# Differential attention: the roots of the output norm reach all partitions through a row in DRAM instead of through TensorE, and the last two pairs of a head are normed in the next head

## What is computed

```
a = (p1 - lam * p2).astype(v.dtype)
o = jnp.einsum("bhqk,bhkd->bhqd", a, v)
...
y = xf * lax.rsqrt(jnp.mean(xf * xf, axis=-1, keepdims=True) + NORM_EPS)
o = rms_norm(o, subln_w) * (1.0 - lam_init)
```

## Time and profile before

| | |
|---|---|
| time, median of 3 runs | 3609.38 us (3599.21 to 3609.42) |
| the profiled execution, its own time | 3618.67 us |
| its span | 3616.9 us |
| mean granted TensorE clock | 0.964 of full speed |
| PE matmul busy | 3342.2 us (92%) |
| PE weight loads busy | 3084.3 us (85%) |
| DVE busy | 1868.7 us (52%) |
| ACT busy | 1185.8 us (33%) |
| POOL busy | 942.6 us (26%) |

### The profile page before, as it was taken

One profiled execution on the slowest core, in us unless ns is written; L12 is line 12 of the kernel. 1 busy time (PEld: TensorE's weight loads), 2 busy tenths in 40 slices (PEclk: granted clock), 3 DMA queues, 4 the chain that ended last, 5 costly groups with the idle time before them and its releaser, 6 DMA issues. The chain is left out here.

```text
span 3616.9 us, 51583 instructions
## 1 busy us (share of the span) xinstructions
PE 3342.2 (92%) x20797; PEld 3084.3 (85%) x20797; DVE 1868.7 (52%) x2655; ACT 1185.8 (33%) x2106; POOL 942.6 (26%) x726
## 2 busy tenths in 40 slices
PE   5898898998889999999988999999798999999997
PEld 4777777887789999999988777777598999999996
DVE  4555555555155554555545555565416545555454
ACT  3334344444232222122223555555413121222111
POOL 1122112222233322223233121221133322332221
PEclk8999999998899999999999999999899999999998
DMA  6333343113211111111112111101231111111101
GB/s 240 108 107 113 112 125 116 51 40 121 87 42 47 41 53 35 41 37 39 54 38 78 38 30 26 35 23 35 97 99 58 42 36 41 41 37 56 35 29 59
DMA packets 206659, 229.78 MB, mean 64 GB/s; under 512 B 30564, under 2 KB 173533, under 8 KB 205341
## 3 DMA queue, kind: packets, MB, share of 16 engines
q1 hardware_dynamic: 186973, 162.69, 14.8%
q10 hardware_dynamic: 11664, 42.47, 3.5%
q0 software_dynamic: 7856, 22.29, 1.7%
HBM read 181.79 MB, written 31.98 MB: 59 GB/s over the span
## 5 line engine op out<-in xcount | busy, mean ns | idle before, releaser
L205 PE MATMUL psum<-Hh,wh 128*128 128x384 f32 x3360 | 1142.2, 340 | 52.6 <-ACT Hh L377 14.7
L206 PE MATMUL psum<-Hh,wl 128*128 128x384 f32 x3360 | 1131.0, 337 | 0.0
L207 PE MATMUL psum<-Hl,wh 128*128 128x384 f32 x3360 | 1130.9, 337 | 0.0
L286 DVE SCALAR_TENSOR_TENSOR x<-psum,mod,x 128x384 f32<-128x384 f32 (+2 forms) x768 | 377.4, 514 | 684.6 <-PE psum L207 643.2
L205 PEld LDWEIGHTS psum<-Hh,wh 128*128 128x128 f32 x3360 | 636.6, 189 | 63.3 <-issue 35.5
L206 PEld LDWEIGHTS psum<-Hh,wl 128*128 128x128 f32 x3360 | 636.8, 190 | 0.0
L207 PEld LDWEIGHTS psum<-Hl,wh 128*128 128x128 f32 x3360 | 636.5, 189 | 0.0
L816 POOL TENSOR_TENSOR wl<-wr,wh 128x1024 fp32r<-128x1024 f32 x88 | 219.8, 2498 | 986.6 <-ACT wh L735 986.6
L766 ACT ACTIVATE ff_u<-psum 128x768 f32<-128x768 f32 x88 | 71.6, 814 | 1109.2 <-PE psum L207 1109.2
L205 PE MATMUL psum<-ff_ah,ff_dh 128*128 128x384 f32 x1056 | 365.1, 346 | 29.4 <-POOL ff_al L838 20.7
L964 DVE SCALAR_TENSOR_TENSOR ff_c<-ff_u,par,ff_c 128x1153 f32<-128x1153 f32 x176 | 377.4, 2144 | 15.8 <-DVE ff_c L961 5.2
(11 more groups left out here) (217 smaller groups left out, 4267.8 us busy)
## 6 DMA issues: line engine op xcount, KB each, us to landing
wr<-w_up SPq DMA_DIRECT2D x88, 512.0 KB, 3.9
ff_dr<-w_down SPq DMA_DIRECT2D x22, 1024.0 KB, 6.1
da_mw<-mod_w ACTq DMA_DIRECT2D x40, 512.0 KB, 3.9
wr<-mod_w ACTq DMA_DIRECT2D x40, 512.0 KB, 4.8
wr<-w_qkv_diff SPq DMA_DIRECT2D x24, 512.0 KB, 19.2
x<-x_save SPq DMA_DIRECT2D x16, 576.0 KB, 7.5
in_mw<-mod_w SPq DMA_DIRECT2D x8, 1024.0 KB, 12.2
Hh<-oh_save SPq DMA_DIRECT2D x14, 576.0 KB, 9.8
```

Source lines behind the costliest of these rows:

```text
L205: pe.matmul(out, w_hi, m_hi, start=start, stop=False)
L206: pe.matmul(out, w_lo, m_hi, start=False, stop=False)
L207: return pe.matmul(out, w_hi, m_lo, start=False, stop=stop)
L286: last = dve.scalar_tensor_tensor(g.x[:, m, lo:hi], g.PS[:, bank, lo - n * NB:hi - n * NB], g.mod[:, gate + m, cond:cond + 1], g.x[:, m, l ...
```

## The change

The "BC" products leave TensorE and the list of bank uses. In their place SP issues two transfers for each pair: `spread_out` writes the one or two columns of `r` from 128 partitions into a row of DRAM, token by token (`r_rows`, 4 bytes each), and `spread_in` reads that row of 1024 bytes back into the `y` buffer of every partition. `spread_in` waits until `spread_out` has landed, and SP, which issues in order, waits with it. `normalise` reads `o` and `y` in SBUF and writes `y` in place. The pairs 3 and 4 of a head are normed and stored in step 1 of the next head; those of the last head after its loop. `outputs` on ACT waits for the norm of two pairs before, or for the whole head before it in pairs 0 and 1.

```diff
+        g.r_rows = nc.dram_tensor("r_rows", [2, 2, P], F32, kind="Internal").ap()
...
-    PV_AT, ST_AT, BC_AT = {2: [0], 4: [1], 6: [2], 8: [3], 9: [4]}, {3: [0], 5: [1], 7: [2], 9: [3, 4]}, {4: [0], 6: [1], 8: [2], 9: [3, 4]}
+    PV_AT, ST_AT, Y_AT = {2: [0], 4: [1], 6: [2], 8: [3], 9: [4]}, {3: [0], 5: [1], 7: [2], 9: [3, 4]}, {5: [0], 7: [1], 9: [2]}
...
-            last = tiles + [("PV", 4), ("ST", 3), ("ST", 4)] + [("W+",)] * ahead2 + [("BC", 3), ("BC", 4)]
+            last = tiles + [("PV", 4), ("ST", 3), ("ST", 4)] + [("W+",)] * ahead2
...
-        u += [("BC", p) for p in BC_AT.get(s, [])]
...
+            def spread_out(h, p):
+                n, done = PAIRS[p][1], len(PAIRS) * h.index + p
+                sp.wait_ge(b.r_d, done + 1)
+                if done >= 2:
+                    sp.wait_ge(b.r_in, 16 * (done - 1))
+                sp.dma_start(g.r_rows[done % 2, 0:n].rearrange("i q -> q i"), b.r[:, p, 0:n],
+                             allow_slow_non_contiguous=True).then_inc(b.r_out, 16)
+
+            def spread_in(h, p):
+                n, done = PAIRS[p][1], len(PAIRS) * h.index + p
+                sp.wait_ge(b.r_out, 16 * done + 16)
+                sp.wait_ge(b.y_split, max(2 * (done - 1), 0) + Y0)
+                sp.dma_start(b.y[:, done % 2, 0:n * P],
+                             g.r_rows[done % 2, 0:n].rearrange("i q -> (i q)").partition_broadcast(P)).then_inc(b.r_in, 16)
...
                 if not ahead:
                     sp.wait_ge(b.y_out, 32 * len(PAIRS) * (HEADS - 1) + 16)
                     load_outputs(g, sp, b)
+                    for p in range(3):
+                        spread(h, p)
+                    spread_end(h)
                     return
                 load_w(after(h, 1), "v")
                 cached_keys(after(h, 1))
                 swap_keys(after(h, 1), ring)
+                spread(h, 0)
                 if ahead2:
                     load_w(after(h, 2), "k")
                 new_keys(after(h, 1), ring)
+                spread(h, 1)
                 swap_queries(after(h, 1), ring)
+                spread(h, 2)
                 if ahead2:
                     load_w(after(h, 2), "q")
+                spread_end(h)
...
             def outputs(ring, h, p):
                 n = PAIRS[p][1] * P
-                if p >= 2:
-                    ring.wait_read(act, free, ("BC", p - 2))
+                if h.index or p >= 2:
+                    act.wait_ge(b.y_d, len(PAIRS) * h.index + p - (1 if p else 0))
...
-                elif what == "BC":
-                    p = use[1]
-                    pe.wait_ge(b.r_d, len(PAIRS) * h.index + p + 1)
-                    for i in range(PAIRS[p][1]):
-                        last = pe.matmul(out[:, i * P:(i + 1) * P], b.r[:, p, i:i + 1].to_broadcast([P, P]), g.ident[:, :],
-                                         start=True, stop=True)
...
             def normalise(ring, h, p):
-                n, use = PAIRS[p][1] * P, ("BC", p)
-                dve.wait_ge(b.full, ring.done(use))
-                dve.wait_ge(b.y_split, 2 * (len(PAIRS) * h.index + p) + Y0 - 2)
-                dve.scalar_tensor_tensor(b.y[:, (h.odd + p) % 2, 0:n], b.o[:, p % 2, 0:n], b.wsub[:, :], PS[:, ring.bank(use), 0:n],
-                                         ALU.mult, ALU.mult).then_inc(free[ring.bank(use)], 1)
+                n, done = PAIRS[p][1] * P, len(PAIRS) * h.index + p
+                if ring is not None:
+                    ring.wait_read(dve, free, ("PV", p))
+                dve.wait_ge(b.r_in, 16 * done + 16)
+                y = b.y[:, done % 2, 0:n]
+                dve.scalar_tensor_tensor(y, b.o[:, p % 2, 0:n], b.wsub[:, :], y, ALU.mult, ALU.mult).then_inc(b.y_d, 1)
...
+                    if s == 1 and h.index:
+                        for p in (3, 4):
+                            normalise(None, after(h, -1), p)
```

More of the change, by code:

```diff
@@ L1203, in phase_diff_attention @@
         "tab w_in w_hi w_lo free0 free1 ahead mw_in coef full s_mm nmax exp prob rope kswap qswap"
-        " ck_in cv_in ko_out v_out r_d y_out sub soft y_split wo_in0 wo_in1 wo_hi wo_lo o_in", reused=True)
+        " ck_in cv_in ko_out v_out r_d r_out r_in y_d y_out sub soft y_split wo_in0 wo_in1 wo_hi wo_lo o_in", reused=True)
     free = {WORK: b.free0, WORK + 1: b.free1}
@@ L1305, in swap_queries, with spread, spread_end @@
                 rope_swap(sp, b.rot[:, :], b.q[:, 0:NS], b.qswap)
+            def spread_out(h, p):
[11 more added lines that the diff above has]
+                             g.r_rows[done % 2, 0:n].rearrange("i q -> (i q)").partition_broadcast(P)).then_inc(b.r_in, 16)
+            def spread(h, p):
+                spread_out(h, p)
+                spread_in(h, p)
+            def spread_end(h):
+                spread(h, 3)
+                spread(h, 4)
             def first(ring):
@@ L1465, in root, with store @@
                 pool.tensor_tensor(b.r[:, p, 0:n], b.ms[:, p, 0:n], g.half[:, 0:n], ALU.pow).then_inc(b.r_d, 1)
-            def store(ring, h, p, last):
-                ring.wait_read(pool, free, ("BC", p))
-                store_output(g, pool, b, h.index, p, last, b.y[:, (h.odd + p) % 2, :], Y0)
+            def store(h, p):
+                pool.wait_ge(b.y_d, len(PAIRS) * h.index + p + 1)
+                store_output(g, pool, b, h.index, p, h.index == HEADS - 1, b.y[:, (h.odd + p) % 2, :], Y0)
             def first(ring):
@@ L1483, in body @@
                         root(ring, p)
-                    for p in BC_AT.get(s - 1, []):
-                        store(ring, h, p, not ahead)
+                    for p in Y_AT.get(s, []):
+                        store(h, p)
+                    if s == 1 and h.index:
+                        for p in (3, 4):
+                            store(after(h, -1), p)
                     if ahead and s in (1, 4):
@@ L1491, in body @@
                         first_out_weights_lo(g, pool, b, s - 2)
-                for p in BC_AT[STEPS - 1]:
-                    store(ring, h, p, not ahead)
             heads(pool, first, body)
+            for p in (3, 4):
+                store(after(HEAD0, HEADS - 1), p)
             pool.wait_ge(b.y_split, 2 * len(PAIRS) * HEADS + Y0)
@@ L1695, in body @@
                     add_mod_bias(g, dve, h.index + 1, PS[:, ring.bank(("MT",)), :]).then_inc(free[ring.bank(("MT",))], 1)
-                for p in BC_AT[TILES - 1]:
+                for p in Y_AT[TILES]:
                     normalise(ring, h, p)
@@ L1701, in body @@
                     maxima(after(h, 1), 0)
-                for p in BC_AT[TILES]:
-                    normalise(ring, h, p)
             heads(dve, first, body)
+            for p in (3, 4):
+                normalise(None, after(HEAD0, HEADS - 1), p)
             for i in range(1, 4):
```

## The result

The changed kernel takes 3806.53 us (median of 4 runs, 3802.3 to 3809.18), the kernel before 3606.07 on the same chip (4 runs, 3599.21 to 3609.42): a ratio of 1.0557, 95% interval 1.0537 to 1.0578. It is 200 us slower, where a gain of 22 us was forecast.

A forecast was written before the change was run, and what follows sets the result against it. PE was taken to bound heads 0 to 6, sharing head 7 with the loop over maxima and exponentials; 27.3 + 0.6 - 5.0 - 0.5 = 22.4 us saved, so 3587 us from a median of 3609.4, range 3576 to 3603.

The forecast's parts named there:

- the price of the store: A pair's store of roots to DRAM: 1.7 us as for a 64 KB store plus 0.7 for packets, 2.4 us.
- The read: Reading 128 KB of roots back into all partitions: 2.1 us, as the 128 KB store takes.
- Hiding of pairs 0 to 2: In heads 0 to 4 their two transfers, 4.5 us, hide within a step of 12 us.
- The chain of pairs 3 and 4: At a head's end their transfers run in a row; pair 4's roots are there 8.5 us after `da_ms` of pair 3.
- slower than before: Rival: slow transfers at head ends, into head 7 and at phase end; over 10.8 us slower needs L = 4.3; chance 0.08.
- 1.5 + 3L: When pair 4's roots are there at a head's end, with L the time of each of three chained transfers.
- Its slope: Beyond the rival's limit, 8 us of time for each us of chain, at head ends, into head 7 and phase end.
- its threshold of 11.1: Roots there up to 11.1 us (L = 3.2) cost time only at the step into head 7 and phase end.
- What leaves PE: 144 matmuls and the waits that go with them, over all heads: 27.3 us saved.
- M's waits for its slices: M, the slice's matmuls on PE: in pair 0 most of 1.1 us freed ends in waiting; 0.3 us gained.
- that of step 6: PE's idle before the slice's matmuls in step 6 of heads 0 to 4: longer, about 3.7 us, on `wr<-mod_w`.
- At the end of the phase: After the last head nothing covers the transfers: 10.2 us in place of 5.2, cost 5.0 us.

The follow-up runs named there:

- far store: Changed kernel with roots written 512 bytes apart in DRAM and one row of an input read instead of the roots: 3587.64 us.
- the groups: Changed kernel with 16 roots side by side in 64 bytes, such groups 512 bytes apart, and a row of norm weights read instead: 3601.73 us.
- another row read: Changed kernel with all stores as in the change, but the read takes a row of the output norm's weights: 3742.34 us.
- the turned kernel: Changed kernel with DVE turning roots into runs of 128 bytes before storing, pairs 3 and 4 both stored before either read: 3603.83 us, ratio 1.0002.
- both edits: Changed kernel with roots written 512 bytes apart and each partition reading an input row of its own: 3583.48 us, ratio 0.9946.

## Why the prediction was wrong

**The step that failed** is the price of the store: "It is nearest to the first, since nothing else is under way at these places, so I take 1.7 + 0.7 = 2.4 us out". It measured 9.3 and 10.4. Both bounds (1.7 and 3.8) were rows of other stores, whose packets don't crowd a short row, and the term that was added, 46 ns a packet, takes the packets as spread over 16 engines. The far store's 1.6 us fits that (256 packets in a row at 46 ns would be 11.8 us), but here they also meet at their target: 128 to each 512 bytes. By the groups (8 packets to a stretch, 1.8 us) and the full row (9.1) it is (9.1 - 1.8) / 120 = 61 ns, an estimate, for each packet that must wait. Pair 4's store, 128 packets to one such stretch, gives less: 7.4 us with another row read against 2.9 far apart, (7.4 - 2.9) / 120 = 38 ns. So neither a fixed price for a packet nor 512 bytes as the length that counts is shown, and no number of packets between 8 and 128 was tried. The mechanism inside the memory was not seen; that packets to one stretch wait for each other is inferred from the landing times.

The Trainium skill, page DMA: Bandwidth & Descriptors, Specifications, says that transfers under 512 bytes are read, modified and written. The runs neither show nor exclude that as the reason for the waiting; taken as a price of every short packet it would have missed too, since with far targets the same packets cost nothing that shows.

**The read** was taken as 2.1 us. With a row for each partition and far stores it is that; with one row for all and far stores 3.0 to 3.1; behind stores in the full row 3.4 with rows of their own, 3.5 with another row for all, and 5.2 with the row just stored. Why was not tested.

**Hiding of pairs 0 to 2.** "A step takes 12 us against 4.5 us for the two transfers": 9.3 + 5.2 = 14.5 us and the issue don't fit. With pairs 0 to 2 alone in the full row the phase is 62 us longer, with pairs 3 and 4 alone 102, with all 149, and the read of the full row adds 71: 149 + 71, or 221 us from unrounded ends, over the far writes.

**The chain of pairs 3 and 4** was laid out rightly: the rival "slower than before" named its mechanism and "1.5 + 3L". With the 9.4, 11.5 and 3.8 of the timeline in place of 3L it gives 26.2; the trace has 26.1. Its slope, 8 us of time for each us, comes out near: with pairs 3 and 4 in the full row the chain was 20.7 us, with far writes 8.95, and (20.7 - 8.95) x 8 = 94 of the 101.6 measured. That it is so near may be luck in part: PE was also busy 722 us there for the products of 704, at a clock of 0.91 against 0.96, for which the slope has no term. Wrong was its chance, 0.08, since it hung on a price for which no row stood near, and its threshold of 11.1: in heads 1 to 4, where a slice's copy stands behind the norms (4 waits, 58.6 us), PE doesn't ask for the exponentials first but for the bank that the slice's copy must empty. In the turned kernel a copy at 441.46 held PE 1.4 us, so it was wanted 9.0 us behind `da_ms`. That wait was in no step of the prediction.

**What leaves PE** was taken at 27.3 us and is 22.3 (14 to 26), without transfers. With the transfers at 1.6 and 2.1 us the gain is 20.6, where 22.4 were forecast. That the two are near is in part luck: the gain was taken too high, and the cost of the transfers too (27.3 + 0.6 - 22.4 = 5.5 us, where 22.3 - 20.6 = 1.7 show, a difference inside the scatter). At the end of the phase, pair 3's `da_ms` to the MEMSET took 12.1 us before and 15.1 with both edits, 3.0 more, where 5.0 were taken. M's waits for its slices came to 20.6 us in 15 up to 690 us (both edits, the longest 2.6), and to 26.7 in 16 before: that of step 6, forecast at about 3.7, didn't grow.

## What to carry to other kernels

To move a number from each partition into a row by DMA, ask where the small packets land, not only how many there are: pack them into runs first (one DVE turn of 0.2 us). Spreading them in DRAM makes the store as cheap, but here it only ran with another row read: what it costs to read spread roots back was not tried. A round trip through DRAM belongs where its whole length is covered, and is priced in a place like its own; if no row of the trace resembles the transfer, the range must reach far. And what stands behind a waiting instruction on its engine includes the banks that it will empty.

## What the hardware showed that was not expected

- 128 packets of 4 bytes to 512 bytes of DRAM land in 6.9 to 10.4 us, 256 packets to 1 KB in 8.6 to 9.4; the same packets 64 or 512 bytes apart in 1.6 (pair 4's, behind another read, in 1.9 to 2.9).
- 128 partitions reading one row of 1 KB take 3.0 to 3.1 us where rows of their own take 2.1, and 5.2 just behind such a store of that row, but 3.0 behind a store of few runs.
- Issuing on SP takes 0.3 to 0.6 us a DMA, and 1.60 us for three stores in a row, as long as a far store takes from issue to landing (1.6).
- Where PE waited more, its granted clock was lower: 0.86 over the phase of the change, 0.96 with far writes, and the same products kept it busy 746 us in place of 704.
